# Whole tiles for the 16 left-over keys, and two heads side by side in the weighted sums of a stick-breaking attention

## The chip, the core and the metric

The kernel runs on one core of a Trainium2 chip. The metric is the device time of one execution in microseconds (us); lower is better. Engines are named as in the profile: PE is TensorE's matrix products, PEld its weight loads, DVE is VectorE, ACT is ScalarE, POOL is GpSimd and SP is SyncE.

## What is computed

The whole program is a small two-layer trunk: 16 learned meta tokens are put before 1024 positions, a gated delta-rule layer and a SwiGLU layer follow, then one shared key/value projection, a layer of stick-breaking attention with 16 heads of 64, another SwiGLU layer and a last norm. The change touches the attention alone:

```python
z = jnp.einsum('bhqd,bhkd->bhqk', q_blk, k) * scale          # 16 heads, L = 1040 keys
log_beta = jax.nn.log_sigmoid(z)
log_keep = jnp.where(visible, log_beta - z, 0.0)             # visible: key before query
log_w = log_beta + lax.cumsum(log_keep, axis=3, reverse=True) - log_keep
w = jnp.where(visible, jnp.exp(log_w), 0.0)
return jnp.einsum('bhqk,bhkd->bhqd', w, v)
```

The kernel uses that the weight of a key is a difference of two neighbouring products of "keep" factors. So it forms the running product P of sigmoid(-z) from the last key backwards, and sums P against differences of neighbouring values plus a bias, which gives the same output.

## The kernel before

**Units.** A pair is two heads (128 rows of channels). There are 8 pairs (`PAIRS`). Each pair has 16 units (`NU`): two heads h and 8 query blocks i of 128, in the order `UNITS`: for big in 7, 6, 5, 4, for each head, block big and then block 7 - big. So units with an even number are big and those with an odd number small. A unit has 16 + 128 (i + 1) keys: i + 1 whole blocks of 128 and 16 keys left over.

**What a unit goes through.** PE forms the scores of the unit (`scores`, three units ahead; lines L2025 and L2026 for the low and high parts of the keys, L2028 for the mask). ACT takes the sigmoid of them from PSUM (`kept`, L1112, into the tile kp). DVE scans kp into Pr (`scan`, L1589, a running product). PE turns Pr over, in blocks of 128 (`turn`, L2059 for whole blocks, L2061 for the 16 keys left over: an ordinary product with 16 columns of weights that moves the last 32 columns of the identity). ACT copies the turned blocks from PSUM banks 4 and 5 into PT (`take_turned`, L1122). PE sums them against the differences of the values in dV (`weigh`, L2078 for whole blocks, L2076 and L2081 for the 16 keys, with 16 rows), into bank 6 or 7. dV holds for each block 256 columns: head 0's 64, 128 zeros, head 1's 64. Each head multiplies with 128 columns of it, of which 64 are zeros, so both heads add into the same 128 partitions of the bank. When a half of the pair's 1024 queries is done, DVE adds the bias and takes it out (`outputs`, L1630).

**fp32 products.** Each fp32 product (L2059 excepted, which is a transposition) appears in the trace as two load and two product instructions.

**Order on PE.** `slot(U)` writes it out: turn the first group of unit U, scores of U + 3, turn the second group, weigh unit U - 1, turn the third group, and in three slots of each pair turn the next pair's values (L2044). Before slot 0 come the scores of units 0 to 2 and the last job of the query projection. ACT, DVE and POOL each have their own queue in order; semaphores tie them together (`t_z` scores, `t_kp` sigmoid, `t_p` scan, `t_tr` turned group, `t_ca` group copied, `t_pv` unit weighed, `t_ot` output taken, `t_zero` zeroing done).

**POOL.** Once a pair it splits the last result into a high part (L802) and a low part (L804), forms the differences of the next values (`value_steps`, L778 to L781), and makes the low parts of the next keys and queries for each head (`split_keys`, L765 and L767), which wait for ACT's high parts (L1094, L1095). ACT makes those after units 3 and 7. Before the first unit POOL stores the last query projection (L785), waits for all stores and zeroes the middle of dV (L797).

Of the kernel before, what the change touches and what calls it, by code (L numbers as in the profile page):

```python
# [20 lines left out]
META = 16  # L21
# [104 lines left out]
def trunk(nc, x, meta_tokens, gdn_norm_g, gdn_w_in, gdn_conv_w, gdn_a_log, gdn_dt_bias, gdn_onorm_g,  # L126
# [17 lines left out]
    with ctx:  # L144
# [49 lines left out]
        with ExitStack() as a:  # L194
            def att_x(name, shape, dt=F32):
                return a.enter_context(nc.sbuf_tensor(name, shape, dt))
            dvT0 = att_x("dvT0", [128, L])
            with ExitStack() as b:
                kraw0 = [b.enter_context(nc.sbuf_tensor(f"krawp{i}", [128, L], F32)) for i in range(2)]
            KL0 = [att_x(f"KLp{i}", [128, L], F32R) for i in range(2)]  # L200
            KH0 = [att_x(f"KHp{i}", [128, L], F32R) for i in range(2)]
            PrX0 = att_x("PrX0", [128, L])
# [7 lines left out]
            PrX1 = att_x("PrX1", [128, 528])  # L210
            att_x("bpad", [128, 288])
# [31 lines left out]
        with ExitStack() as a:  # L243
            def att(name, shape, dt=F32):
                return a.enter_context(nc.sbuf_tensor(name, shape, dt))

            def key_query(tag):

                with ExitStack() as b:
                    kr = [b.enter_context(nc.sbuf_tensor(f"kraw{tag}{i}", [128, L], F32)) for i in range(2)]  # L250
                return (kr, [att(f"KL{tag}{i}", [128, L], F32R) for i in range(2)],
                        [att(f"KH{tag}{i}", [128, L], F32R) for i in range(2)],
                        [att(f"QS{tag}{i}", [128, SEQ], F32R) for i in range(2)])
            oT = att("oT", [128, SEQ])
            kpS1 = att("kpS1", [128, 528])
            kpB0 = att("kpB0", [128, L])
            set_e = key_query("e")
            kpS0 = att("kpS0", [128, 528])
            PTb = att("PTb", [128, 1056])
            att("tpad", [128, 400])  # L260
# [3 lines left out]
            PrB = [att(f"PrB{i}", [128, L]) for i in range(2)]  # L264
            PrS = [att(f"PrS{i}", [128, 528]) for i in range(2)]
            kpB1 = att("kpB1", [128, L])
            PTs = att("PTs", [128, 544])
        gpad = keep("gpad", [128, 2 * L + 512])

        with ExitStack() as a:  # L270
# [93 lines left out]

            return dV12[j % 2] if j else dV0

        def kp_of(U):

            return ((kpB0, kpB1), (kpS0, kpS1))[U % 2][U // 2 % 2]

        def Pr_of(U):

            return (PrX0, PrX1)[U] if U < 2 else (PrB, PrS)[U % 2][U // 2 % 2]

        def PT_of(U):

            return (PTb, PTs)[U % 2]

        def q_bank(m, ch):

# [204 lines left out]
        def _(pool):  # L585
# [197 lines left out]
            for m in range(P_Q.jobs):  # L783
                pool.wait_ge(taken, TAKEN0[P_Q] + 2 * (m + 1))
                pool.dma_start(s_q[m], obuf[:, m % 2, 0:SEQ]).then_inc(stored[m % 2], 16)  # L785
                if m == 3:
                    pool.memset(dV0[:, :, 64:192], 0.0).then_inc(t_zero, 1)
                    value_steps(0)
                if m == 4:
                    split_keys(0, 0)  # L790
                if m == 5:
                    split_keys(0, 1)
            for b in range(2):
                pool.wait_ge(stored[b], 16 * 28)
            pool.wait_ge(mm_chunk, P_O.mm0)
            for d in dV12:
                pool.memset(d[:, :, 64:192], 0.0).then_inc(t_zero, 1)  # L797

            def result(j):

# [16 lines left out]
        def _(act):  # L817
# [286 lines left out]
            def kept(U):  # L1104

                z0, n = z_place(U)
                act.wait_ge(t_z, U + 1)
                if U == 3:
                    act.wait_ge(taken, TAKEN0[P_O])
                if U > 3:  # L1110
                    act.wait_ge(t_p, U - 3)
                act.activation(kp_of(U)[:, 0:n], PSf[:, z0:z0 + n], ACT.Sigmoid, scale=-0.125).then_inc(t_kp, 1)  # L1112

            def take_turned(U, g):

                k0, nb = TURNS[UNITS[U % NU][1]][g]
                n = TURN_NO["P", U, g]
                w = 128 * nb + (32 if n == last_turn(U) else 0)
                act.wait_ge(t_tr, n + 1)
                if U > 1:  # L1120
                    act.wait_ge(t_pv, U - 1)
                act.activation(PT_of(U)[:, 128 * k0:128 * k0 + w], PS[:, 4 + n % 2, 0:w], ACT.Copy).then_inc(t_ca, 1)  # L1122

            def take_values(j, g):

                k0, nb = V_PARTS[g]
                n = TURN_NO["V", j, g]
                rows = META if g == 2 else 128
                act.wait_ge(t_tr, n + 1)
                act.wait_ge(t_zero, 1 if j == 0 else 3)  # L1130
                if j > 2:
                    act.wait_ge(t_pv, NU * (j - 1))
# [52 lines left out]
        def _(dve):  # L1185
# [434 lines left out]

            def outputs(j, ch):

                dve.wait_ge(t_pv, NU * j + 16 - ch)
# [27 lines left out]
        def _(pe):  # L1651
# [396 lines left out]
            def turn(U, g):  # L2048

                i = UNITS[U % NU][1]  # L2050
                k0, nb = TURNS[i][g]
                n = TURN_NO["P", U, g]
                if n < 5:
                    pe.wait_ge(taken, TAKEN0[P_Q] + 2 * P_Q.jobs - 4 + n)
                pe.wait_ge(t_ca, n - 1)
                pe.wait_ge(t_p, U + 1)
                P = Pr_of(U)
                for k in range(nb):
                    m = pe.transpose(PS[:, 4 + n % 2, 128 * k:128 * k + 128], P[:, 128 * (k0 + k):128 * (k0 + k) + 128], ident[:, :])  # L2059
                if n == last_turn(U):  # L2060
                    m = pe.matmul(PS[0:META, 4 + n % 2, 128 * nb:128 * nb + 32], P[:, 128 * (i + 1):128 * (i + 1) + META],  # L2061
                                  ident[:, 96:128], start=True, stop=True)
                m.then_inc(t_tr, 1)

            def weigh(U):

                j, u = divmod(U, NU)
                h, i = UNITS[u]
                V, P = dV_of(j), PT_of(U)
# [13 lines left out]
                m.then_inc(t_pv, 1)  # L2083

            def slot(U):
# [102 lines left out]
```

## Time and profile before

| what | value |
|---|---|
| median of 3 runs | 3294.31 us (3293.29 to 3294.46) |
| the profiled execution | 3292.72 us |
| its span, first to last instruction | 3291.1 us |
| PE busy | 3196.3 us, 97% |
| DVE, ACT, POOL busy | 1601.5, 887.3, 657.0 us |
| mean granted TensorE clock | 0.993 |
| attention stage | 2035.8 to 2432.9 us |

The profile is that of one execution. Its matrix products are pipelined, and the ends of their records are modelled: a product of 128 columns has a record of some 0.27 us, though the next can start 0.11 us after it. What tells the pace is the distance from start to start.

### The profile page before, as it was taken

The numbers are of one execution on the slowest core, as the hardware profiler recorded it, in microseconds if no ns is written. First come the engines' busy times: TensorE is split into PE (matmuls) and PEld (weight loads), VectorE is DVE, ScalarE is ACT, GpSimd is POOL, SyncE is SP. The second block draws the span as 40 slices with busy tenths as digits, with TensorE's granted clock in tenths as the row PEclk, the third lists the DMA queues.
The fourth block names the chain that finished last, engine by engine and source line by source line (L and its number), as shares of the span: only waits on it lengthen the run. The fifth ranks groups of instructions, "written<-read, shape, count | busy, mean of one in ns | idle before, by whom it ended". The sixth has DMA issues, their size and how long they took to land.

```text
span 3291.1 us, 47938 instructions
## 1 busy us (share of the span) xinstructions
PE 3196.3 (97%) x19632; PEld 2904.9 (88%) x19632; DVE 1601.5 (49%) x2016; ACT 887.3 (27%) x1418; POOL 657.0 (20%) x558
## 2 busy tenths in 40 slices
PE   7999989999999999999998999999999999999998
PEld 6999978888899999999998997888888777777776
DVE  5777456666543334433345333676644334333343
ACT  3211245555421111111112002555532111111112
POOL 3000145555220100000002003344302000000000
PEclk9999999999999999999999999999999999999999
DMA  3333311111111111111111233212201111111111
GB/s 93 91 93 95 105 61 48 53 53 32 49 58 45 45 45 45 38 51 45 45 45 52 91 109 104 59 40 66 52 16 62 45 45 45 51 45 45 51 38 64
DMA packets 196954, 190.38 MB, mean 58 GB/s; under 512 B 7595, under 2 KB 171580, under 8 KB 196812
## 3 DMA queue, kind: packets, MB, share of 16 engines
q1 hardware_dynamic: 188748, 158.60, 16.4%
q0 software_dynamic: 8064, 29.76, 2.7%
q8 instruction: 105, 1.72, 0.2%
q14 instruction: 37, 0.30, 0.0%
HBM read 154.35 MB, written 33.98 MB: 57 GB/s over the span
## 4 chain that ended last, share of the span: by engine, by line
PE 95%; DVE 2%; ACT 2%; issue 1%; POOL 0%; DMA 0%; SPq 0%; ACTq 0%; DVEq 0%; POOLq 0%
PE PS L1659 18%; PE PS L1661 18%; PE PS L1660 18%; PE PS L1977 5%; PE PS L1975 5%; PE PS L1976 5%; PE PS L2078 5%; PE PS L1796 3%; PE PS L2059 2%; PE PS L1805 2%; PE PS L2025 1%; PE PS L2026 1%; PE PS L1812 1%; PE PS L1765 1%; PE PS L2076 1%
## 5 line engine op out<-in xcount | busy, mean ns | idle before, releaser
L1659 PE MATMUL PS<-YH,WL 128*128 128x348 f32 (+1 forms) x3040 | 1040.9, 342 | 14.8 <-DVE hT L1522 14.1
L1660 PE MATMUL PS<-YL,WH 128*128 128x348 f32 (+1 forms) x3040 | 1038.3, 342 | 0.0
L1661 PE MATMUL PS<-YH,WH 128*128 128x348 f32 (+1 forms) x3040 | 1037.4, 341 | 0.0
L1659 PEld LDWEIGHTS PS<-YH,WL 128*128 128x128 f32 x3040 | 571.5, 188 | 61.1 <-DVE hT L1522 19.0
L1660 PEld LDWEIGHTS PS<-YL,WH 128*128 128x128 f32 x3040 | 571.2, 188 | 37.4 <-issue 1.0
L1661 PEld LDWEIGHTS PS<-YH,WH 128*128 128x128 f32 x3040 | 572.4, 188 | 35.6
L749 POOL TENSOR_TENSOR gact<-gact,rs 128x346 f32<-128x346 f32 (+2 forms) x110 | 118.9, 1081 | 1326.3 <-ACT gact L1041 1326.3
L1522 DVE TENSOR_TENSOR hT<-PS,hT 128x346 f32<-128x346 f32 (+2 forms) x440 | 251.9, 586 | 189.2 <-PE PS L1977 189.2
L1975 PE MATMUL PS<-AH,WL 128*128 128x346 f32 (+2 forms) x880 | 310.4, 353 | 12.8 <-DVE AL L1512 6.4
L1976 PE MATMUL PS<-AL,WH 128*128 128x346 f32 (+2 forms) x880 | 310.3, 353 | 0.0
L1977 PE MATMUL PS<-AH,WH 128*128 128x346 f32 (+2 forms) x880 | 310.3, 353 | 0.0
L1047 ACT ACTIVATE AH<-aact 128x1040 fp32r<-128x1040 f32 (+1 forms) x44 | 47.0, 1067 | 866.2 <-DVE aact L1509 866.2
L1189 DVE TENSOR_TENSOR WL<-raw,WH 128x1024 fp32r<-128x1024 f32 x204 | 250.2, 1244 | 46.4 <-ACT WH L821 44.9
L1509 DVE TENSOR_TENSOR aact<-PS,gact 128x346 f32<-128x346 f32 (+2 forms) x110 | 64.7, 588 | 419.4 <-PE PS L1661 419.4
L1975 PEld LDWEIGHTS PS<-AH,WL 128*128 128x128 f32 x880 | 166.6, 189 | 29.2 <-issue 7.1
L1589 DVE TENSOR_TENSOR_SCAN PrB<-kpB 128x912 f32<-128x912 f32 (+3 forms) x63 | 156.4, 2482 | 73.1 <-ACT kpB L1112 73.1
L1977 PEld LDWEIGHTS PS<-AH,WH 128*128 128x128 f32 x880 | 166.8, 190 | 15.7
L1976 PEld LDWEIGHTS PS<-AL,WH 128*128 128x128 f32 x880 | 166.8, 189 | 15.7
L1499 DVE TENSOR_TENSOR gact<-PS,rs 128x346 f32<-128x346 f32 (+2 forms) x110 | 64.5, 586 | 223.8 <-PE PS L1661 223.7
L821 ACT ACTIVATE WH<-raw 128x1024 fp32r<-128x1024 f32 x148 | 150.8, 1047 | 33.1 <-DMA raw<-in_ffn_w_gate_up 30.4
L1041 ACT ACTIVATE gact<-gact 128x346 f32<-128x346 f32 (+2 forms) x110 | 60.4, 549 | 321.8 <-DVE gact L1499 321.6
L666 POOL TENSOR_TENSOR LT<-NT,lvl 104x416 f32<-104x416 f32 x120 | 132.0, 1125 | 0.0
(273 smaller groups left out, 4406.2 us busy)
## 6 DMA issues: line engine op xcount, KB each, us to landing
raw<-in_ffn_w_gate_up SPq DMA_DIRECT2D x88, 512.0 KB, 3.7
raw<-in_ffn_w_down SPq DMA_DIRECT2D x44, 512.0 KB, 3.6
s_in<-obuf POOLq DMA_DIRECT2D x32, 520.0 KB, 4.4
raw<-in_gdn_w_in SPq DMA_DIRECT2D x32, 512.0 KB, 4.0
Xqk<-s_in SPq DMA_DIRECT2D x10, 832.0 KB, 4.3
s_kv<-obuf POOLq DMA_DIRECT2D x16, 520.0 KB, 4.1
raw<-in_w_kv SPq DMA_DIRECT2D x16, 512.0 KB, 4.0
qraw<-s_q SPq DMA_DIRECT2D x32, 256.0 KB, 6.7
```

The costliest lines, as they stand in the source:

```text
L666: pool.tensor_tensor(by_head(LT[g][:, (k - 1) % LTB, :]), by_head(NT[c % 2][g][:, :]), lvl[:, k, :].unsqueeze(1).broadcast_to([C, HG, C]), ...
L821: act.activation(WH[s][:, :], raw[s][:, :], ACT.Copy).then_inc(w_hi, 1)
L1189: dve.tensor_tensor(WL[s][:, :], raw[s][:, :], WH[s][:, :].bitcast(F32), ALU.subtract).then_inc(w_lo, 1)
L1522: dve.tensor_tensor(dst, PS[:, banks[u % len(banks)], 0:n], dst, ALU.add).then_inc(d_add, 1)
L1589: dve.tensor_tensor_scan(Pr_of(U)[:, 0:n][:, ::-1], kp, kp, 1.0, ALU.mult, ALU.bypass).then_inc(t_p, 1)
L1659: pe.matmul(PS[:, bank, 0:n], wl, xh, start=(k == 0), stop=False)
L1660: pe.matmul(PS[:, bank, 0:n], wh, xl, start=False, stop=False)
L1661: m = pe.matmul(PS[:, bank, 0:n], wh, xh, start=False, stop=(k == KT - 1))
L1975: pe.matmul(bank, wl, ah, start=(t == 0), stop=False)
L1976: pe.matmul(bank, wh, al, start=False, stop=False)
L1977: y = pe.matmul(bank, wh, ah, start=False, stop=(t == 1))
L2078: m = pe.matmul(PS[:, bank, c0:c0 + 128], V[:, k, 128 * h:128 * h + 128], P[:, 128 * k:128 * k + 128], start=(h == 0 and k == 0), stop=(h ...
```

## The change

It has four parts. In `turn` the 16 keys left over are transposed as a whole block of 128 (the tiles P are now 640 and 1152 columns wide, so that it exists; only 16 rows and 32 columns of the result are used, which `take_turned` copies by an instruction of its own). In `weigh` the two heads of a query block are taken together, once the second head's unit is there: 64 calls instead of 128. Head h is a column tile of 64 at `tile_position` (0, 64 h), with 64 columns of weights, and writes 64 partitions; the heads alternate for each key block. The left-over keys are summed there with all 128 rows of dV and PT, whose rows beyond 16 POOL has zeroed. `slot` calls `weigh` only for U - 1 of 2 and 3 modulo 4. kp and Pr become one tile, scanned in place, and PT gets a buffer for each head.

```diff
         def take_turned(U, g):
-                w = 128 * nb + (32 if n == last_turn(U) else 0)
                 act.wait_ge(t_tr, n + 1)
-                if U > 1:
-                    act.wait_ge(t_pv, U - 1)
-                act.activation(PT_of(U)[:, 128 * k0:128 * k0 + w], PS[:, 4 + n % 2, 0:w], ACT.Copy).then_inc(t_ca, 1)
+                if U > 3:
+                    act.wait_ge(t_pv, U // 4 * 2 - 1 + U % 2)
+                if n == last_turn(U):
+                    act.wait_ge(t_zero, 6)
+                    act.activation(PT_of(U)[0:META, tail_of(U):tail_of(U) + 32], PS[0:META, 4 + n % 2, 128 * nb + 96:128 * nb + 128], ACT.Copy)
+                act.activation(PT_of(U)[:, 128 * k0:128 * (k0 + nb)], PS[:, 4 + n % 2, 0:128 * nb], ACT.Copy).then_inc(t_ca, 1)
...
         def kept(U):
-                if U == 3:
-                    act.wait_ge(taken, TAKEN0[P_O])
                 if U > 3:
-                    act.wait_ge(t_p, U - 3)
-                act.activation(kp_of(U)[:, 0:n], PSf[:, z0:z0 + n], ACT.Sigmoid, scale=-0.125).then_inc(t_kp, 1)
+                    act.wait_ge(t_tr, last_turn(U - 4) + 1)
+                act.activation(P_of(U)[:, 0:n], PSf[:, z0:z0 + n], ACT.Sigmoid, scale=-0.125).then_inc(t_kp, 1)
...
         def scan(U):
                 dve.wait_ge(t_kp, U + 1)
-                if U > 3:
-                    dve.wait_ge(t_tr, last_turn(U - 4) + 1)
-                kp = kp_of(U)[:, 0:n][:, ::-1]
-                dve.tensor_tensor_scan(Pr_of(U)[:, 0:n][:, ::-1], kp, kp, 1.0, ALU.mult, ALU.bypass).then_inc(t_p, 1)
+                P = P_of(U)[:, 0:n][:, ::-1]
+                dve.tensor_tensor_scan(P, P, P, 1.0, ALU.mult, ALU.bypass).then_inc(t_p, 1)
...
         def turn(U, g):
                 if n == last_turn(U):
-                    m = pe.matmul(PS[0:META, 4 + n % 2, 128 * nb:128 * nb + 32], P[:, 128 * (i + 1):128 * (i + 1) + META],
-                                  ident[:, 96:128], start=True, stop=True)
+                    m = pe.transpose(PS[:, 4 + n % 2, 128 * nb:128 * nb + 128], P[:, 128 * (i + 1):128 * (i + 2)], ident[:, :])
...
         def weigh(U):
                 pe.wait_ge(t_ca, last_turn(U) + 1)
-                if u < 2 and j:
-                    pe.wait_ge(t_ot, 4 * j - 2 + 2 * u)
+                if u < 4 and j:
+                    pe.wait_ge(t_ot, 4 * j - 2 + 2 * (u % 2))
                 for k in range(i + 1):
-                    if h and k == i:
-                        pe.matmul(PS[:, bank, c0 + 96:c0 + 128], V[0:META, i + 1, 128:256], P[0:META, 128 * i + 128:128 * i + 160],
-                                  start=False, stop=False)
-                    m = pe.matmul(PS[:, bank, c0:c0 + 128], V[:, k, 128 * h:128 * h + 128], P[:, 128 * k:128 * k + 128],
-                                  start=(h == 0 and k == 0), stop=(h == 1 and k == i))
-                if not h:
-                    m = pe.matmul(PS[:, bank, c0 + 96:c0 + 128], V[0:META, i + 1, 0:128], P[0:META, 128 * i + 128:128 * i + 160],
-                                  start=False, stop=False)
+                    for h in range(2):
+                        pe.matmul(PS[64 * h:64 * h + 64, bank, c0:c0 + 128], V[:, k, 192 * h:192 * h + 64],
+                                  P[h][:, 128 * k:128 * k + 128], start=(k == 0), stop=False, tile_position=(0, 64 * h))
+                for h in range(2):
+                    m = pe.matmul(PS[64 * h:64 * h + 64, bank, c0 + 96:c0 + 128], V[:, i + 1, 192 * h:192 * h + 64],
+                                  P[h][:, r0:r0 + 32], start=False, stop=True, tile_position=(0, 64 * h))
                 m.then_inc(t_pv, 1)
...
         def slot(U):
-                if U:
+                if U and (U - 1) % 4 > 1:
                     weigh(U - 1)
```

On POOL, the zeroing before the attention now also covers the last 32 columns of the four PT tiles and the whole last block of each dV, and it comes before the wait for the stores. The waits for `t_pv` in `take_values` and `outputs` count 8 weighings a pair instead of 16.

## Rows read from the trace of the kernel before

**Rows 1.** The page: the span, and the chain that ended last.

```profile
span 3291.1 us, 47938 instructions
...
PE 95%; DVE 2%; ACT 2%; issue 1%; POOL 0%; DMA 0%; SPq 0%; ACTq 0%; DVEq 0%; POOLq 0%
```

**Rows 2.** Stretches: us; busy PE, PEld, DVE, ACT, POOL (instructions); clock, DMA share, GB/s.

```profile
2278.80:2328.50 49.70, 49.70 (x365) 41.29 (x364) 33.20 (x21) 26.79 (x52) 20.03 (x10) 1.00 0.23 52
...
2378.20:2432.90 54.70, 54.70 (x399) 45.49 (x399) 28.09 (x24) 26.32 (x52) 3.44 (x2) 1.00 0.09 23
```

**Rows 3.** Waits, 2079.8 to 2378.2 us: us in total, times, longest.

```profile
DVE oT L1630 <- PE PS L2078: 27.3, 6, 4.6
```

**Rows 4.** PE in order of time: start, us, line, operation, tiles, shape, count.

```profile
2294.06 0.44 PE L2059 MATMUL PS<-ident,PrB 128*128 128x128 f32 x2
...
2294.59 0.33 PE L2059 MATMUL PS<-ident,PrS 128*128 128x128 f32 x1
2294.85 0.23 PE L2061 MATMUL PS<-ident,PrS 128*16 128x32 f32 x2
2295.01 0.50 PE L2025 MATMUL PS<-KLo,QSo 128*128 128x512 f32 x1
2295.35 0.39 PE L2026 MATMUL PS<-KHo,QSo 128*128 128x512 f32 x1
2295.58 0.34 PE L2025 MATMUL PS<-KLo,QSo 128*128 128x400 f32 x1
...
2296.01 1.78 PE L2078 MATMUL PS<-PTb,dV 128*128 128x128 f32 x14
2297.72 0.40 PE L2076 MATMUL PS<-PTb,dV 16*128 16x32 f32 x2
2298.05 0.49 PE L2078 MATMUL PS<-PTb,dV 128*128 128x128 f32 x2
```

**Rows 5.** The weight loads of the same stretch.

```profile
2294.85 0.11 PEld L2061 LDWEIGHTS PS<-ident,PrS 128*16 128x16 f32 x2
...
2295.94 1.65 PEld L2078 LDWEIGHTS PS<-PTb,dV 128*128 128x128 f32 x14
```

**Rows 6.** Order of time on PE at the value block of 16.

```profile
2322.69 0.27 PE L2044 MATMUL PS<-ident,dvT 128*16 128x128 f32 x1
2322.80 0.60 PE L2059 MATMUL PS<-ident,PrB 128*128 128x128 f32 x4
```

**Rows 7.** Order of time on PE in the first layer.

```profile
641.58 1.63 PE L1863 MATMUL PS<-osq,ones 128*128 128x416 f32 x4
643.05 0.88 PE L1812 MATMUL PS<-ident,U 104*104 104x104 f32 x8
```

**Rows 8.** Order of time on DVE and POOL, undisturbed first, then together.

```profile
2037.11 2.33 DVE L1589 TENSOR_TENSOR_SCAN PrB<-kpB 128x1040 f32<-128x1040 f32 x1 [1.60 <-ACT kpB L1112]
2039.35 0.43 DVE L1589 TENSOR_TENSOR_SCAN PrS<-kpS 128x144 f32<-128x144 f32 x1
...
2044.42 1.92 POOL L778 TENSOR_TENSOR dvT<-vT 128x1039 f32<-128x1039 f32 x1 [2.72 <-DMA vT<-s_kv]
...
2289.83 1.06 POOL L802 CAST XH<-oT 128x1024 fp32r<-128x1024 f32 x1 [23.40 <-DVE oT L1630]
2290.97 2.35 POOL L804 TENSOR_TENSOR XL<-oT,XH 128x1024 fp32r<-128x1024 f32 x1
2291.26 3.98 DVE L1589 TENSOR_TENSOR_SCAN PrB<-kpB 128x912 f32<-128x912 f32 x1 [1.20 <-ACT kpB L1112]
2293.29 3.67 POOL L778 TENSOR_TENSOR dvT<-vT 128x1039 f32<-128x1039 f32 x1
...
2299.57 2.40 POOL L765 TENSOR_TENSOR KLe<-krawe,KHe 128x1040 fp32r<-128x1040 f32 x1
2302.05 2.66 POOL L767 TENSOR_TENSOR QSe<-qraw,QSe 64x1024 fp32r<-64x1024 f32 x1
```

**Rows 9.** Instruction groups by shape from 2278.8 to 2328.5 us.

```profile
L1122 ACT ACTIVATE PTs<-PS 128x160 f32<-128x160 f32 x5 | 1.5, 301 | 0.0
```

More of the change, by code:

```diff
@@ L201, in trunk @@
             KH0 = [att_x(f"KHp{i}", [128, L], F32R) for i in range(2)]
-            PrX0 = att_x("PrX0", [128, L])
+            att_x("ppad", [128, L])
             vT = att_x("vT", [128, L])
@@ L254, in trunk @@
             oT = att("oT", [128, SEQ])
-            kpS1 = att("kpS1", [128, 528])
-            kpB0 = att("kpB0", [128, L])
+            att("rpad", [128, 16])
+            PB = [att("PB0", [128, 1152]), None]
+            att("epad", [128, 400])
             set_e = key_query("e")
-            kpS0 = att("kpS0", [128, 528])
-            PTb = att("PTb", [128, 1056])
-            att("tpad", [128, 400])
+            Psm = [att("PS0", [128, 640]), None]
+            PTb = [att("PTb0", [128, 1056]), None]
+            att("tpad", [128, 288])
             set_o = key_query("o")
@@ L263, in trunk @@
             dV12 = [att(f"dV{i}", [128, 9, 256]) for i in range(2)]
[L264 to L267, printed above, removed]
+            PB[1] = att("PB1", [128, 1152])
+            Psm[1] = att("PS1", [128, 640])
+            PTb[1] = att("PTb1", [128, 1056])
+            PTs = [att(f"PTs{i}", [128, 544]) for i in range(2)]
         gpad = keep("gpad", [128, 2 * L + 512])
@@ L365, in dV_of, with P_of, tail_of @@
             return dV12[j % 2] if j else dV0
[L367 to L373, printed above, removed]
+        def P_of(U):
+            return (PB, Psm)[U % 2][U // 2 % 2]
         def PT_of(U):
-            return (PTb, PTs)[U % 2]
+            return (PTb, PTs)[U % 2][U // 2 % 2]
+        def tail_of(U):
+            return 512 if U % 2 else 1024
         def q_bank(m, ch):
@@ L786, in _ @@
                 if m == 3:
-                    pool.memset(dV0[:, :, 64:192], 0.0).then_inc(t_zero, 1)
+                    pool.memset(dV0[:, 0:8, 64:192], 0.0).then_inc(t_zero, 1)
+                    pool.memset(dV0[:, 8, :], 0.0).then_inc(t_zero, 1)
                     value_steps(0)
@@ L792, in _ @@
                     split_keys(0, 1)
+            pool.wait_ge(mm_chunk, P_O.mm0)
+            for h in range(2):
+                pool.memset(PTb[h][:, 1024:1056], 0.0).then_inc(t_zero, 1)
+                pool.memset(PTs[h][:, 512:544], 0.0).then_inc(t_zero, 1)
+            for d in dV12:
+                pool.memset(d[:, 0:8, 64:192], 0.0).then_inc(t_zero, 1)
+                pool.memset(d[:, 8, :], 0.0).then_inc(t_zero, 1)
             for b in range(2):
                 pool.wait_ge(stored[b], 16 * 28)
-            pool.wait_ge(mm_chunk, P_O.mm0)
-            for d in dV12:
-                pool.memset(d[:, :, 64:192], 0.0).then_inc(t_zero, 1)
             def result(j):
@@ L1129, in take_values @@
                 act.wait_ge(t_tr, n + 1)
-                act.wait_ge(t_zero, 1 if j == 0 else 3)
+                act.wait_ge(t_zero, 2 if j == 0 else 10)
                 if j > 2:
-                    act.wait_ge(t_pv, NU * (j - 1))
+                    act.wait_ge(t_pv, NU // 2 * (j - 1))
                 act.activation(dV_of(j)[0:rows, k0:k0 + nb, :].rearrange("p k (q c) -> p k q c", c=64)[:, :, 0:4:3, :],
@@ L1621, in outputs @@
             def outputs(j, ch):
-                dve.wait_ge(t_pv, NU * j + 16 - ch)
+                dve.wait_ge(t_pv, NU // 2 * j + 8 - ch)
                 if j:
@@ L2056, in turn @@
                 pe.wait_ge(t_p, U + 1)
-                P = Pr_of(U)
+                P = P_of(U)
                 for k in range(nb):
@@ L2067, in weigh @@
                 j, u = divmod(U, NU)
-                h, i = UNITS[u]
-                V, P = dV_of(j), PT_of(U)
+                i = UNITS[u][1]
+                V, P, r0 = dV_of(j), (PT_of(U - 2), PT_of(U)), tail_of(U)
                 bank, c0 = 6 + i // 4, 128 * (i % 4)
                 pe.wait_ge(t_ca, last_turn(U) + 1)
-                if u < 2 and j:
-                    pe.wait_ge(t_ot, 4 * j - 2 + 2 * u)
+                if u < 4 and j:
+                    pe.wait_ge(t_ot, 4 * j - 2 + 2 * (u % 2))
                 for k in range(i + 1):
-                    if h and k == i:
-                        pe.matmul(PS[:, bank, c0 + 96:c0 + 128], V[0:META, i + 1, 128:256], P[0:META, 128 * i + 128:128 * i + 160],
-                                  start=False, stop=False)
-                    m = pe.matmul(PS[:, bank, c0:c0 + 128], V[:, k, 128 * h:128 * h + 128], P[:, 128 * k:128 * k + 128],
-                                  start=(h == 0 and k == 0), stop=(h == 1 and k == i))
-                if not h:
-                    m = pe.matmul(PS[:, bank, c0 + 96:c0 + 128], V[0:META, i + 1, 0:128], P[0:META, 128 * i + 128:128 * i + 160],
-                                  start=False, stop=False)
+                    for h in range(2):
+                        pe.matmul(PS[64 * h:64 * h + 64, bank, c0:c0 + 128], V[:, k, 192 * h:192 * h + 64],
+                                  P[h][:, 128 * k:128 * k + 128], start=(k == 0), stop=False, tile_position=(0, 64 * h))
+                for h in range(2):
+                    m = pe.matmul(PS[64 * h:64 * h + 64, bank, c0 + 96:c0 + 128], V[:, i + 1, 192 * h:192 * h + 64],
+                                  P[h][:, r0:r0 + 32], start=False, stop=True, tile_position=(0, 64 * h))
                 m.then_inc(t_pv, 1)
```

3 lines of the change are left out of this document (1 added, 2 removed).

## The prediction

> **What bounds the kernel now.** I read the page first: the chain that ended last is 95% TensorE (PE) over a span of 3291.1 us, so no other engine sets the end [rows 1]. The profiled execution took 3292.7 us, 1.6 less than the median of 3294.3 us, and the sum below is made against the former. Then I cut out the attention stage, which is all that the diff touches. One pair of heads lasts 49.7 us; PE is busy for all 49.7 of it, VectorE (DVE) for 33.2, ScalarE (ACT) for 26.8, GpSimd (POOL) for 20.0, and the granted clock is 1.00, the upper level of 2.4 GHz [rows 2]. Eight such pairs fill the time from 2035.8 to 2432.9 us. In the list of waits PE waits for nobody there; DVE waits for PE, about 4.6 us once a pair, before it takes the sums out [rows 3]. So a nanosecond less on PE is a nanosecond less of time, until the next engine is in the way. The second row there is the last pair, in which POOL prepares nothing for a next one.
>
> A busy PE need not be PE at its peak, so I went on to single starts on PE. A plain value product of 128 columns of weights goes every 0.112 us: 14 loads in 1.65 us, the last 0.19 long [rows 4, 5]. The short products for the 16 left-over keys are the surprise. On the value side, from 2296.01 to 2298.05 there are 14 plain products and one tail of two 32-column instructions: 2.04 us, where 14 x 0.112 is 1.57. The next two products take 0.49 us to the end of the last, whose record is 0.27 long, so the step between them is 0.22 instead of 0.11. Of these 0.58 us some 0.05 belongs to the mask product ahead; 0.53 is the tail's. Where transpositions follow, the exit is 0.05 cheaper (two in 0.44, less the last one's 0.27, is 0.17 instead of 0.11), so the mean is 0.5 us [rows 4]. On the transposition side one transposition with its 128*16 tail takes 0.42 us instead of 0.11, of which some 0.05 comes from the tail before; the 512-column product behind it takes 0.34 instead of 0.23. That is about 0.36 us a tail [rows 4]. Two instructions of 16 weight columns are only 0.04 us of work, so each of the two changes of shape costs about 0.16 us. A transposition with 16 columns of weights pays nothing: the next starts 0.11 us later [rows 6]. It is the change of array shape by an ordinary product that costs, not the small operand.
>
> **The change, part by part.** There are 128 units (8 pairs x 2 heads x 8 query blocks).
>
> Turned tails: 128 x 0.36 = 46 us go, 128 whole transpositions at 0.11 = 14 us come. Gain 32 us.
>
> Value tails: 128 x 0.5 = 64 us go. In their place stand 64 weighings, each entering and leaving the two-tile shape: 2 x 0.16 = 0.32 us. Each also holds four short tail instructions (two heads, two passes of the fp32 product). Loads of 16 columns stand 0.015 us apart (two in 0.11, one 0.09) and those of 128 stand 0.112 [rows 5], so I take 0.056 for 64 columns, 0.22 us for the four. 64 x 0.54 = 35 us. Gain 29 us.
>
> Value products: 8 x 72 x 2 = 1152 instructions before and after, 129 us at 0.112. No row shows two column tiles at once. The upper bound is that they run one after another. Streaming 128 fp32 columns costs about 0.11 us whatever is loaded: 416 fp32 columns take 1.47/4 = 0.37 us, while 512 columns of the rounded type take 0.23 [rows 4, 7]. Then nothing is gained. The lower bound is that two stream together and the loads set the pace, 0.056 us each by the estimate above, so 64.5 us go. I take the lower one: outputs and weight columns of the two heads are disjoint, the loads balance it exactly, and the end hardly depends on it, as the next part shows.
>
> TensorEngine Tiling (Array Packing) of the Trainium skill, section Key Properties, says that changing the tiling mode drains the array, while different tiles run in parallel. Its first half agrees with the 0.16 us above; the second no run here shows. By it the products are worth the 64.5 us, by the serial row 0; and a change of tile inside a weighing costs nothing.
>
> On PE that is 32 + 29 + 64.5 = 126 us, 15.7 a pair: 49.7 becomes 34.0. Without overlap it is 61 us, 7.6 a pair: 42.1.
>
> **What is late next.** A scan of 1040 columns takes 2.33 us and one of 144 takes 0.43, so 2.12 ns a column plus 0.12. The 2 x 8 scans of a pair (9472 columns) need 22.1 us. Scans and POOL's operations exclude each other. The scan of 912 columns needs 2.05 us by that rate; it is issued at 2291.26, lasts 3.98, and ends 2.0 us after POOL's subtraction ends at 2293.32. POOL's next one needs 1.92 us alone, but lasts 3.67 when queued behind that scan [rows 8]. POOL's own work a pair is 2.35 + 1.9 + 2 x 2.4 + 2 x 2.66 + 1.06 + about 0.6 = 16 us [rows 8] (1.06 is the conversion, 0.6 my estimate of its three small operations; what is left of the 20.0 busy in [rows 2] are waits for scans). Together 38.1 us, and 39.6 with the 1.5 us in which DVE takes sums out. That is the floor once PE needs only 34.0. Scores run only three units before their transpositions, so idle time of one side is not all made up later. I take 40.0 us for each of the six middle pairs, a gain of 9.7, together 58 us. The first has neither the 3.4 us of result conversion nor its first two scans: gain 11 (34.0 plus some 4 of waits). The last has POOL nearly empty: gain 13 (34.0 plus 2 to 3 of waits). 82 us in all.
>
> SBUF — State Buffer of the Trainium skill, section SBUF: two separate sides, says that GpSimd and a VectorE operation with two SBUF inputs hold a shared port exclusively, for a whole instruction. The trace agrees: a scan of 2.05 us lasts 3.98. It speaks against the change: by it about 44 of the 126 us that PE saves come to nothing.
>
> Costs that I set at nothing. ACT gets one more copy of 32 columns for each unit. A copy of 160 columns takes 0.30 us [rows 9]; 0.2 by the least, so net 2.7 us a pair, 29.5 of 40: hidden beside PE and DVE. Queued behind it are the main copy, and PE's transposition two banks on. In the slots that no longer hold a weighing (two of four) PE has only scores to cover the copy; I count up to 0.4 us there, in the 40.0 and the first and last pair's waits. Ridding the kernel of separate scan outputs moves a wait: the sigmoid now waits for the transpositions of four units earlier, which PE has done a slot before. The new zeroing of the tails comes ahead of the zeroing of dV on POOL and is small; ACT's first tail copy needs it at about 2038.5 us. If it is late, that costs some 1 us once. The longer weighings delay DVE's taking out of sums by less than the 4.6 us that it now waits.
>
> **The rivals.**
> A (my forecast): PE at 34, DVE and POOL bound the middle pairs. 3292.7 - 82 + 1.6 = 3212 us. For it: full use of PE, the port rows. By the bounds of the middle pairs, 38.5 to 43 us, it is 3203 to 3230. Chance 0.58.
> B: the two tiles don't overlap. PE at 42.1 is above the floor; 42.5 with small waits, 7.2 x 8 = 58 us: 3236 us, 3229 to 3245. For it: no row shows overlap, and fp32 products take two passes. Against it: nothing in the trace. 0.25.
> C: the port binds less, because POOL's operations fall where PE has DVE idle anyway, or its records overstate them. A pair takes 36 us, 13.7 x 8 = 110: 3184 us. Against it: 22.1 + 16 has to be placed in it. 0.08.
> D, the other side: each change of tile inside a weighing costs like a change of shape. A pair has 36 key blocks and 8 tails, each with a step to the other head and one back, so 88 changes; at 0.16 us they cost 14.1 us against 7.6 gained: a pair takes 56.2 us, and the time is 3294.3 + 8 x 6.5 = 3346 us. It decides from 7.6/88 = 0.086 us a change. For it: the rows price a change at twice that. Against it: the array keeps its shape between the two heads. 0.06.
> The remaining 0.03 is for a wait that I don't see that takes it all.
>
> **How the numbers follow.** The forecast is A's 3212 us. A and B together hold 0.83, so the range reaches from a little below A's lower bound to B's upper bound: 3195 to 3245 us. A measurement here tells no less than about 0.2% (6.6 us) from no change. Faster by more: A, B, C and a little more, 0.93; within: 0.01; slower: D, 0.06.
>
> **What would show it.** Transposition tails gone as a shape, one more transposition of 128 for each unit at 0.11 us. Value products: starts of both heads in pairs and 0.056 us apart in the mean (A), or 0.11 (B), or over 0.16 (D). One gap of some 0.1 us before and after each of 64 weighings. PE waits for scans, 5 us a pair in the middle pairs under A, next to none under B. DVE near or over 33 us busy in 40. The period of a middle pair is 40.0 (A), 42.5 (B), 36 (C). I am wrong if PE waits for ACT's copies in the slots without a weighing, far above 0.4 us each, or if the granted clock falls below 1.00 once PE has waits in it.

## The result, and the profile after

The changed kernel takes 3194.45 us (median of 4 runs, 3194.15 to 3194.66) against 3294.39 us of the kernel before on the same chip: 0.9697 of it, with a 95% interval of 0.968 to 0.9714. That is 99.9 us less. The forecast was 3212 us, in a range from 3195 to 3245: the direction held, and what came to bind the middle pairs was what I had foretold, though it cost less than I had put it at. The time lies 0.55 us below the range.

The page of the changed kernel, its span and its chain, to be laid beside [rows 1]:

```profile
span 3192.5 us, 47692 instructions
...
PE 89%; DVE 6%; ACT 2%; issue 1%; DMA 1%; POOL 0%; SPq 0%; ACTq 0%; DVEq 0%; POOLq 0%
```

DVE now has 6% of the chain, where it had 2%. Two stretches of the changed kernel, a middle pair and the last, with the columns of [rows 2]:

```profile
2186.20:2223.40 37.20, 34.09 (x347) 28.48 (x347) 34.09 (x20) 26.51 (x69) 24.90 (x10) 1.00 0.31 74
...
2297.90:2333.00 35.10, 32.48 (x338) 27.21 (x340) 27.00 (x22) 23.65 (x66) 5.14 (x2) 1.00 0.14 33
```

A middle pair takes 37.2 us instead of 49.7. PE and DVE are both busy for 34.1 of them (for DVE that includes its waits for POOL), so neither works without a gap: they hand the wait to and fro. Cut at the first transposition of a pair, the stage compares as follows (starts from the order of time on PE; the last pair ends with the last sums taken out):

| stretch | before | after | gain | forecast gain |
|---|---|---|---|---|
| first pair | 51.1 | 42.3 | 8.8 | 11 |
| six middle pairs | 6 x 49.7 | 6 x 37.2 | 75 | 58 |
| last pair | 48.9 | 35.1 | 13.8 | 13 |

The products of the value sums on PE in order of time, which answer to [rows 4]:

```profile
2197.05 0.34 PE L2029 MATMUL PS<-KHe,QSe 128*128 128x400 f32 x1
2197.23 0.23 PE L2031 MATMUL PS<-maskb,identb 128*128 128x128 bf16 x1
2197.39 1.97 PE L2078 MATMUL PS<-PTb,dV 128*64 128x128 f32 x32
2199.18 0.26 PE L2081 MATMUL PS<-PTb,dV 128*64 128x32 f32 x4
2199.37 0.33 PE L2062 MATMUL PS<-ident,PB 128*128 128x128 f32 x1
```

There are 32 products in 1.97 us, the last record 0.28 long: 0.055 us a product, half of the 0.112 of [rows 4, 5]. The first comes 0.16 us after the mask product, where it came 0.07 after it in [rows 4] with no change of shape (the row of 2296.01 and the load of 2295.94): 0.09 for going into column tiles. The four tail instructions and the way out take 0.19 us together.

DVE and POOL of the changed kernel in order of time, which answer to [rows 8]:

```profile
2195.06 2.06 DVE L1592 TENSOR_TENSOR_SCAN PB<-PB 128x912 f32<-128x912 f32 x1 [0.73 <-ACT PB L1115]
2197.03 2.83 DVE L1592 TENSOR_TENSOR_SCAN PS<-PS 128x272 f32<-128x272 f32 x1
2199.79 3.70 DVE L1592 TENSOR_TENSOR_SCAN PB<-PB 128x912 f32<-128x912 f32 x1
2203.41 0.69 DVE L1592 TENSOR_TENSOR_SCAN PS<-PS 128x272 f32<-128x272 f32 x1
2204.03 1.76 DVE L1592 TENSOR_TENSOR_SCAN PB<-PB 128x784 f32<-128x784 f32 x1
```

```profile
2194.10 1.06 POOL L807 CAST XH<-oT 128x1024 fp32r<-128x1024 f32 x1 [12.00 <-DVE oT L1633]
2195.24 4.04 POOL L809 TENSOR_TENSOR XL<-oT,XH 128x1024 fp32r<-128x1024 f32 x1
2199.24 2.34 POOL L778 TENSOR_TENSOR dvT<-vT 128x1039 f32<-128x1039 f32 x1
2201.55 1.96 POOL L779 TENSOR_SCALAR dvT<-vT 128x1 f32<-128x1 f32 x1
2203.46 0.64 POOL L780 COPY bias<-vT 128x8 f32<-128x8 f32 x1
2204.04 1.73 POOL L781 COPY bias<-vT 128x8 f32<-128x8 f32 x1
```

They take turns, as foretold: the subtraction of 2195.24 doesn't get on before the scan ends at 2197.12, the next scan waits for it until 2199.28, and so on. And PE waits for it:

```profile
2202.28 0.23 PE L2031 MATMUL PS<-maskb,identb 128*128 128x128 bf16 x1
2203.64 0.41 PE L2062 MATMUL PS<-ident,PB 128*128 128x128 f32 x2 [1.12 <-DVE PB L1592]
```

The transposition needs the scan that ends at 2203.49, 3.70 us after its issue. But two things in the rows of DVE and POOL were not in my sum. An operation that had to wait takes 0.12 to 0.2 us less once it may run than it takes alone: the subtraction ends 2.16 us after the scan (alone 2.35), the next ends 1.7 us after its scan (alone 1.92), the scan of 2199.79 ends 1.91 us after the subtraction (alone 2.05). I read it as its start overlapping the other's end. And the three small operations hold nobody up: they wait for scans themselves (those of 2201.55, 2203.46 and 2204.04 each end within 0.02 us of a scan), but the scans of 2203.41 and 2204.03 run at their own pace with a POOL operation in flight.

The conversion does take turns. It starts at 2194.10, in the middle of a scan that lasts from 2193.88 to 2194.33, and ends 0.83 us after that scan; in a kernel of the experiments below (two of POOL's operations twice) one starts with no scan in flight and takes 1.04 us, and the scan that is issued in the middle of it ends 1.91 us after it:

```profile
2205.30 1.04 POOL L811 CAST XH<-oT 128x1024 fp32r<-128x1024 f32 x1 [10.34 <-DVE oT L1640]
2205.94 2.31 DVE L1599 TENSOR_TENSOR_SCAN PB<-PB 128x912 f32<-128x912 f32 x1 [0.73 <-ACT PB L1122]
```

In the changed kernel it costs next to nothing all the same, as DVE waits 0.73 us for ACT's sigmoid just then, from 2194.33 to 2195.06.

### The profile page after: what moved, and what is told of

Same layout as the page of the kernel before. It is cut to its first block, busy times and chain, and to the rows that moved or that the text cites. A ratio compares the mean times of both kernels' runs of the same rounds, so it can differ in the third digit from the quotient of the medians.

```text
span 3192.5 us, 47692 instructions
## 1 busy us (share of the span) xinstructions
PE 3072.3 (96%) x19504; PEld 2804.0 (88%) x19504; DVE 1606.5 (50%) x2016; ACT 885.2 (28%) x1546; POOL 687.9 (22%) x565
## 4 chain that ended last, share of the span: by engine, by line
PE 89%; DVE 6%; ACT 2%; issue 1%; DMA 1%; POOL 0%; SPq 0%; ACTq 0%; DVEq 0%; POOLq 0%
PE PS L1662 19%; PE PS L1664 19%; PE PS L1663 19%; PE PS L1980 5%; PE PS L1978 5%; PE PS L1979 5%; PE PS L1799 3%; DVE PB L1592 2%; PE PS L1808 2%; DVE PS L1592 2%; PE PS L2062 1%; PE PS L1815 1%; PE PS L2078 1%; PE PS L1768 1%; PE PS L2029 1%
## 5 line engine op out<-in xcount | busy, mean ns | idle before, releaser
L1592 DVE TENSOR_TENSOR_SCAN PB<-PB 128x1040 f32<-128x1040 f32 (+3 forms) x64 | 158.1, 2470 | 20.4 <-ACT PB L1115 20.4
L826 ACT ACTIVATE WH<-raw 128x1024 fp32r<-128x1024 f32 x148 | 150.8, 1047 | 35.1 <-DMA raw<-in_ffn_w_gate_up 32.4
```

Of the source, the lines that this page charges most:

```text
L826: act.activation(WH[s][:, :], raw[s][:, :], ACT.Copy).then_inc(w_hi, 1)
L1592: dve.tensor_tensor_scan(P, P, P, 1.0, ALU.mult, ALU.bypass).then_inc(t_p, 1)
```

## The experiments

Each pair below is a middle pair. The same pieces of the program ahead of the attention ended up to 4 us apart from kernel to kernel, so a few us between kernels are not to be believed without the lengths of the pairs. Every experiment was timed beside the kernel before on its own chip (medians of 3292.9 to 3295.1 us), and the changed kernel again only beside the last group; the first four and the doubled operations have two executions each.

**One head after the other.** The same instructions in another order:

```diff
-                for k in range(i + 1):
-                    for h in range(2):
+                for h in range(2):
+                    for k in range(i + 1):
```

> The changed kernel, but in each weighing all blocks of head 0 come first and then all of head 1; the same instructions, tiles and sums. Theory 1 (the gain of the value products is that two neighbouring instructions for different column tiles stream together): starts 0.11 us apart instead of 0.055 in the mean, 144 x 0.055 = 7.9 us more on PE a pair, PE from 33 to 41, above what else binds; a middle pair goes from 37.2 to about 41.2 us and the time from 3194 to about 3227 us. Rival 1 (64 columns of weights make an instruction cheap by themselves, or PE fetches the other tile's instructions from far ahead): no change, 3194 us.

Measured: 3236.5 us, 0.9827 of before (0.9799 to 0.9856), a middle pair 42.3 us. That is 9 us above the expectation of 3227: PE is busy for 38.8 us of the pair, less than the 41 expected, but 3.5 us of waits stand beside them. The order of time on PE in this kernel:

```profile
2176.89 3.00 PE L2078 MATMUL PS<-PTb,dV 128*64 128x128 f32 x29
2179.62 0.30 PE L2081 MATMUL PS<-PTb,dV 128*64 128x32 f32 x2
2179.72 0.49 PE L2078 MATMUL PS<-PTb,dV 128*64 128x128 f32 x3
2180.05 0.25 PE L2081 MATMUL PS<-PTb,dV 128*64 128x32 f32 x2
```

32 products take 3.16 us, 0.10 each. So the gain of the column tiles is that neighbours in the queue for different tiles stream together; a tile of 64 columns alone is worth next to nothing: away from the seam its starts are 0.109 us apart. The step is a little under 0.11, because around the seam between the heads some still overlap: the tail of head 0, which stands behind all of head 1's blocks in the program, starts before head 1's last three records.

**Without column tiles.** Whole tiles stay for the left-over keys, and so does the new order of the weighings; each head multiplies with 128 columns of weights again:

```diff
-                        pe.matmul(PS[64 * h:64 * h + 64, bank, c0:c0 + 128], V[:, k, 192 * h:192 * h + 64],
-                                  P[h][:, 128 * k:128 * k + 128], start=(k == 0), stop=False, tile_position=(0, 64 * h))
+                        pe.matmul(PS[:, bank, c0:c0 + 128], V[:, k, 128 * h:128 * h + 128],
+                                  P[h][:, 128 * k:128 * k + 128], start=(h == 0 and k == 0), stop=False)
...
-                    m = pe.matmul(PS[64 * h:64 * h + 64, bank, c0 + 96:c0 + 128], V[:, i + 1, 192 * h:192 * h + 64],
-                                  P[h][:, r0:r0 + 32], start=False, stop=True, tile_position=(0, 64 * h))
+                    m = pe.matmul(PS[:, bank, c0 + 96:c0 + 128], V[:, i + 1, 128 * h:128 * h + 128],
+                                  P[h][:, r0:r0 + 32], start=False, stop=(h == 1))
```

> The changed kernel without column tiles: both heads multiply with 128 columns of weights, 64 of them zeros, as before the change; the whole tiles for the left-over keys and the order of the weighings stay. It isolates the first half of the change. By the steps in the traces 144 x 0.112 + 32 x 0.11 = 19.6 us of weighing a pair instead of 11.2, PE 33 + 8.4 = 41.4, a middle pair about 41.6 us, the time about 3230 us. So some 64 of the 100 us would come from the whole tiles alone, and 36 from the column tiles. Rival: the shape changes of the old tails were hidden somewhere and the tails are worth little; then this is near 3270 us.

Measured: 3250.9 us, 0.9871 of before (0.9842 to 0.9899). Its middle pair:

```profile
2169.40:2213.50 44.10, 42.32 (x347) 38.23 (x347) 32.89 (x20) 26.68 (x69) 22.78 (x10) 1.00 0.26 61
```

The whole tiles, with the new order of the weighings, are worth 42 us, and the column tiles 56 more; the expectation had 64 and 36, and 3230 us. PE's own work came out 0.9 us a pair above it, and 1.8 us of waits come on top, most of them of transpositions for ACT's copies. I put them down to the slots that have lost their weighing; that was not tested by itself.

**POOL's subtractions taken away.** For each of the four:

```diff
-                pool.tensor_tensor(KL[b][:, :], kr[b][:, :], KH[b][:, :].bitcast(F32), ALU.subtract).then_inc(t_lo, 1)
+                pool.memset(KL[b][:, :].bitcast(F32), 0.0).then_inc(t_lo, 1)
```

> The changed kernel with POOL's four kinds of subtraction in the attention (low parts of keys, queries and results, differences of values) replaced by zeroing of the same tiles, which reads nothing; that part of the computation is left out. Theory 2 (scans and POOL's operations exclude each other, and this is what middle pairs wait for now): scans have no long records any more, PE waits little, a middle pair about 34 us, 3194 - 6 x 3.2 = 3175 us. Rival 2 (the waits of PE come from ACT's copies and the order of slots): a middle pair stays at 37 us, 3194 us.

Measured: 3181.2 us, 0.9659 of before (0.9631 to 0.9687), 13 us below the changed kernel. Its middle pair:

```profile
2180.00:2215.00 35.00, 33.83 (x347) 28.37 (x347) 23.15 (x20) 26.37 (x69) 7.69 (x10) 1.00 0.32 78
```

DVE falls from 34.1 to 23.2 us busy, without one scan less: 10.9 us of its records were waits for POOL. PE has 33.8 us of work, as forecast (34.0), and 1.2 us idle. So in the changed kernel taking turns costs 2.2 us a middle pair, where the forecast had PE wait for scans for 5.

**Value products taken away.** Only the first key block of each sum is multiplied.

```diff
-                for k in range(i + 1):
+                for k in range(1):
```

> The changed kernel with only the first block of each sum multiplied; the other blocks' value products are left out. PE has 112 x 0.055 = 6.2 us less a pair, 27 instead of 33. Theory 2: the middle pairs are at the port's floor and hardly move: 35 to 37 us, 3180 to 3194 us; what they come to is the floor that I put at 38.1. Rival (PE sets the pace of most of the pair): 31 us a pair, 3145 us.

Measured: 3189.4 us, 0.9684 of before (0.9656 to 0.9712). The middle pairs take 36.3 to 38.8 us, 37.5 in the mean, against 37.2 in the changed kernel. Two of its rows:

```profile
2110.10:2147.40 37.30, 30.96 (x235) 24.85 (x235) 34.60 (x20) 26.76 (x69) 23.47 (x10) 0.91 0.31 72
...
2297.80:2331.70 33.90, 30.50 (x250) 24.25 (x251) 29.33 (x27) 25.95 (x71) 5.08 (x2) 1.00 0.14 34
```

A middle pair doesn't get shorter with less work on PE. It is a weaker proof than it looks: the granted clock of this stretch is 0.91, so PE spent part of it at the lower level of 1.2 GHz, after it had waited. What it shows, as the changed kernel does, is that a pair of 37.3 us is possible with POOL's work in it, so the floor of 38.1 us was no floor. It also shows the conversion taking turns, in every pair:

```profile
2117.15 1.06 POOL L807 CAST XH<-oT 128x1024 fp32r<-128x1024 f32 x1 [13.43 <-DVE oT L1633]
2117.55 2.57 DVE L1592 TENSOR_TENSOR_SCAN PB<-PB 128x912 f32<-128x912 f32 x1 [0.17 <-ACT PB L1115]
```

The scan is issued in the middle of the conversion and ends 1.91 us after it, the same as behind a subtraction.

**Two of POOL's operations twice.**

```diff
+                pool.tensor_tensor(XL[:, j, META:L], oT[:, :], XH[:, j, META:L].bitcast(F32), ALU.subtract).then_inc(t_x, 1)
+                tx[0] += 1
+                pool.wait_ge(t_x, tx[0])
                 pool.tensor_tensor(XL[:, j, META:L], oT[:, :], XH[:, j, META:L].bitcast(F32), ALU.subtract).then_inc(t_ol, 1)
```

(and likewise for the differences of the values)

> The changed kernel with two of POOL's operations done twice in each pair, with the same result: the low part of the result (2.35 us) and the differences of the values (1.9 us). Theory 2 (middle pairs are bound by scans and POOL's operations taking turns): nearly all of the 4.0 us that this adds to their sum shows, a middle pair 41 us, 3194 + 6 x 3.9 = 3218 us. Rival (PE's 33.8 us and the waits for ACT bind, POOL's work is mostly beside it): under 1.5 us a pair, at most 3203 us.

Measured: 3220.6 us (3217.6 and 3223.6), 0.9778 of before (0.9758 to 0.9798). The six middle pairs take 40.3 to 41.5 us, 41.0 in the mean: 3.8 us more for 4.3 us of added work (2.35 and 1.92 alone; 2.16 and 1.7 behind a scan). At the margin, POOL's work in a middle pair is paid nearly in full.

**The second pair's high parts later.** In the changed kernel's first pair ACT stands still ahead of the first conversion of the second pair's keys, and all its later work waits behind it:

```profile
2049.35 1.07 ACT L1099 ACTIVATE KHo<-krawo 128x1040 fp32r<-128x1040 f32 x1 [5.13 <-DMA qraw<-s_q]
```

Three stretches of the changed kernel there show what follows:

```profile
2046.00:2050.00 4.00, 1.05 (x14) 0.77 (x13) 0.31 (x1) 0.65 (x1) 2.49 (x4) 1.00 1.03 220
2050.00:2054.00 4.00, 2.09 (x8) 1.79 (x9) 1.83 (x1) 3.02 (x8) 2.47 (x2) 0.64 1.04 206
2054.00:2058.00 4.00, 4.00 (x18) 3.52 (x18) 3.29 (x2) 2.93 (x7) 2.59 (x1) 0.50 0.18 67
```

PE has next to nothing to do, and then the granted clock falls to the lower level, 0.50 (1.2 GHz), and stays there for 4 us in which PE is busy throughout.

```diff
-                    if u in (3, 7):
-                        split_keys(j + 1, u // 4)
+                    if u in ((3, 7) if j else (7, 10)):
+                        split_keys(j + 1, int(u > (3 if j else 7)))
```

> The changed kernel, in which ACT makes the high parts of the second pair's keys and queries after units 7 and 10 of the first pair instead of 3 and 7. In the first pair of the changed kernel DVE waits 5.9 us for a sigmoid behind ACT's wait for the loads of these keys. Theory 3 (this wait, and the lower clock after it, ate some 5 us of the first pair's gain): the gap goes and the first pair takes 5 to 8 us less, 3187 to 3190 us. Rival (the loads are late whatever waits for them, and the next pair takes up the delay): within 2 us of 3194 us.

Measured: 3190.5 us (3187.6 to 3192.0), 0.9683 of before (0.9667 to 0.97). The first pair goes from 42.3 to 35.9 us, with the clock at 1.00. Of these 6.4 us the time shows 4.0, and this kernel's profile 2.2: its first transposition came 4.2 us later. That lateness is not the edit's work. It is there in the kernel with one head after the other too, which lacks the edit (first transposition at 2040.72 us, against 2036.28 in the changed kernel), and most of it arises long before the attention: from 1720 to 1730 us PE is busy throughout in all three kernels, at a granted clock of 1.00 in the changed kernel and of 0.76 and 0.77 in these two. Why the clock differs there is open.

**Both weighings in one slot.**

```diff
-                if U and (U - 1) % 4 > 1:
-                    weigh(U - 1)
+                if U % 4 == 3:
+                    weigh(U - 1)
+                    weigh(U)
```

> The changed kernel, in which both weighings of four units stand next to each other in the slot of the fourth unit, so that PE changes into column tiles and back once instead of twice: 32 entries and exits of 0.25 to 0.3 us less, 1.1 us a pair. If the middle pairs are bound by scans and POOL (theory 2), nearly nothing shows: 3190 to 3195 us. If PE's own work sets the pace, 3185 us.

Measured: 3202.1 us, 0.9722 of before (0.9706 to 0.9738), 7.7 us more than the changed kernel. Both expectations missed. The change of shape in between does go (the second weighing starts 0.09 us after the first's tails), but a middle pair takes 38.4 us. I put it down to three slots of four that have no weighing under which ACT's copies and DVE's scans can catch up. Two of its waits:

```profile
PEld PS L2062 <- ACT PTb L1127: 15.7, 36, 0.8
...
PEld PS L2062 <- ACT dV L1138: 12.2, 10, 1.4
```

In the changed kernel the first is 10.1 us over six pairs, and the second is not in the list. But a turn is lost as well:

```profile
2198.43 2.36 POOL L809 TENSOR_TENSOR XL<-oT,XH 128x1024 fp32r<-128x1024 f32 x1
2198.44 4.26 DVE L1592 TENSOR_TENSOR_SCAN PB<-PB 128x912 f32<-128x912 f32 x1 [0.93 <-ACT PB L1115]
```

Here the subtraction starts 0.01 us before the scan and goes first, and the scan lasts 4.26 us; in the changed kernel the scan comes first and lasts 2.06. Which of the two makes the 1.2 us was not separated.

**Low parts on DVE.**

```diff
+                if j < PAIRS - 1 and u in (7, 11):
+                    low(j + 1, u // 8)
```

Here `low` holds the two subtractions of `split_keys`, on DVE, and POOL's calls for the later pairs are gone.

> The changed kernel with the low parts of keys and queries of the later pairs made by DVE (after the scans of units 7 and 11) instead of POOL. A subtraction of 1024 columns takes DVE 1.24 us and POOL 2.4 to 2.7 us, so the sum of what excludes each other falls by 10.1 - 5.0 = 5 us a pair, from 33.4 to about 28.5, below PE's 33.8. Theory 2: a middle pair comes near PE's own pace as with the zeroings in place of the subtractions, 35 us, 3194 - 6 x 2.2 = 3181 us. Rival (what counts is DVE's own work, not the exclusion): DVE gets 5 us more to do, a middle pair stays at 37 us or grows, 3194 us or more.

Measured: 3190.1 us, 0.9685 of before (0.9668 to 0.9701), a middle pair 36.5 us: a third of what I expected. The order of time points to a reason. The subtractions that stay on POOL are those that come when PE is closest behind DVE, and the two scans behind them are as long as in the changed kernel:

```profile
2195.12 2.83 DVE L1590 TENSOR_TENSOR_SCAN PS<-PS 128x272 f32<-128x272 f32 x1
2197.88 3.70 DVE L1590 TENSOR_TENSOR_SCAN PB<-PB 128x912 f32<-128x912 f32 x1
```

If so, it is not the sum of the turns that binds the pair, but the two scans behind the result's low part and the value differences. The next version tests it.

**Everything on DVE.** All four subtractions of the later pairs are on DVE: the result's after the scan of unit 5, the value differences after unit 6, the low parts of keys and queries after units 7 and 11 (10 and 13 in the first pair), together with the later high parts. Beside it, the previous kernel with the later high parts alone, and the changed kernel again.

> The changed kernel with all four kinds of subtraction of the later pairs on DVE, which needs 1.2 us for each where POOL needs 1.9 to 2.7, and with the second pair's high parts made later as in e5_late_split. POOL keeps the conversion and three small operations. Theory 2: nothing but scans and DVE's own work is left on the port, so a middle pair comes to the 35.0 us of e3_memsets, and with the first pair's 3 to 5 us the time is 3176 to 3181 us, below the changed kernel and below the kernel before. Rival (a scan that stands behind a subtraction on DVE is as late as one that waits for POOL): 36.5 us as in e9_dve_low, 3187 us.

> e9_dve_low with the second pair's high parts made later as in e5_late_split. If the two gains add (3.9 and 4.3 us), 3186 us; if the 4 us of e5_late_split were scatter from kernel to kernel, 3190 us.

> The changed kernel itself, on the same chip as the two above: 3194 us within 2. The stage ahead of the attention ends between 2022 and 2027 us in the traces so far, for kernels that are the same there; this shows how much of a few us between kernels is worth believing.

Measured, five rounds on one chip:

| kernel | median us | ratio to before | first, middle, last pair |
|---|---|---|---|
| changed kernel again | 3194.43 | 0.9699 (0.9686 to 0.9712) | 40.9, 37.2, 35.1 |
| low parts of keys and queries on DVE, later high parts | 3184.27 | 0.9667 (0.9654 to 0.9681) | 34.8, 36.5, 35.1 |
| all four on DVE, later high parts | 3175.92 | 0.9640 (0.9626 to 0.9653) | 34.8, 35.0, 35.1 |

A middle pair of the last:

```profile
2185.00:2220.00 35.00, 33.83 (x347) 28.36 (x347) 29.45 (x26) 26.33 (x68) 4.82 (x5) 1.00 0.33 77
```

The pair is as short as with the subtractions left out, though they are all done. This version beats both kernels, by 119 and 18.5 us. It does what the expectation said of theory 2, and the rival there (a subtraction on DVE delays a scan as much) is out: it delays it for 1.2 us only. The version changes two things at once, though, the engine of the two remaining subtractions and their place in the order; whether later turns on POOL would have done as well was not tested.

## Why the prediction was right in kind and outside its range

**What bounds the kernel before**: right. PE's own work set the pace of the attention, and each shape change in it was paid.

**PE's work after**: right in sum, 33.8 us a pair in the two kernels without subtractions on POOL against 34.0 forecast, and nearly so in its halves: the left-over keys gave 7.4 us a pair (49.7 to 42.3) where I had 7.6, the value products 8.5 (42.3 to 33.8) where I had 8.1. The four short tail instructions cost less than the 0.22 us that I gave them: with the way out of column tiles they take 0.19.

**Overlap of two column tiles**: right. The lower bound, 0.056 us, was taken and 0.055 measured; the experiment with one head after the other shows that it is the order of the queue that makes it. Rival B is out: it would have needed 42.1 us of PE work a pair. Rival D is out too: no product waits for a change of tile.

TensorEngine Tiling (Array Packing) of the Trainium skill, section Key Properties, says that a change of mode drains the array and that different tiles run in parallel. Both halves are in line with the runs: 0.09 us more on entry, and 0.055 us a product.

**What is late next**: right in kind, and wrong in size. This is the step that failed. I wrote "Together 38.1 us, and 39.6 with the 1.5 us in which DVE takes sums out. That is the floor", and took 40.0 for a middle pair, with 38.5 as the lower bound. It was 37.2. The sum added times that operations take alone, or with a wait in them, and the rows show less. Take for each operation of DVE and POOL in the pair from 2186.20 us only what it adds: from its start, or from the end of the one before it where that is later, to its own end. Then the scans take 20.4 us where I had 22.1, the six subtractions 12.7 where I had 14.4, the conversion 0.8 of 1.06, the small operations nothing where I had 0.6, the taking out of the sums 1.4 of 1.5. That is 35.3 us against the 39.6, and 1.9 us in which neither engine is at work make the 37.2. Whoever stands behind another, of either engine, is 0.1 to 0.2 us quicker: that is most of the scans' and the subtractions' part.

Some of it could be read in [rows 8] before the run. The scan of 2291.26 ends 1.92 us after the subtraction, at 2295.24 against 2293.32; I wrote 2.0, and missed that this is less than the 2.05 it takes alone. The differences behind it end 1.72 us after it, and not 1.92. And the 2.66 us that I took twice as the queries' subtraction have a wait in them: behind a scan in the changed kernel it takes 2.16 to 2.18.

Six pairs at 2.8 us less than forecast are 17 us of the 18 that were missed, and the last pair 0.8; the first pair took back 2.2, and the other 2 lie outside the three rows of the table. And the sum alone doesn't tell the length: counted in the same way it is 31.8 us with the low parts on DVE, but a pair took 36.5, and only the version that also moved the other two subtractions freed the rest. A sum of exclusive work bounds a pair from below; what it costs above PE's time depends on when each turn comes.

**The lower end of the range**: rival C, with the port binding less, was given 36 us a pair and 8%; the truth lies between A and C, nearer to C, and half of C's reason is what the rows bear out: the records overstate what POOL's operations hold. The range left C out and began at 3195 us. That the time came within 0.55 us of it is luck: without the 2.2 us that the first pair lost it would have been further off.

**The first pair**: forecast gain 11, measured 8.8. The wait of ACT for the loads of the second pair, 5.1 us, and the fall of the clock after it were not in the working, though in the kernel before, too, DVE starts no scan from 2046.6 to 2051.9 us. One of my signs of being wrong came true there, and not in the middle pairs: the granted clock fell below 1.00 (0.92 over the first pair) once PE had waits in it.

**The costs set at nothing**: the zeroing on POOL was done by 2037.96 us, in time. ACT's additional copies have records of 0.17 us and stayed beside PE; ACT is busy for 26.5 us of a middle pair, not for 29.5 as forecast. Of the slots without a weighing I wrote up to 0.4 us; with subtractions out of the way all waits of PE in a pair are 1.2 us. The merged weighings cost 1.2 us a pair more, though there a lost turn comes in beside the cover.

## What to carry to other kernels

Put instructions for different column tiles next to each other in the queue; behind one another they gain next to nothing. Keep small left-over products in the array shape of their neighbours, zero-padded, since on PE each change of shape costs more than the padding. When the engine that sets the pace is relieved, look for work of two engines that takes turns, add only what each operation takes behind the other, and look first at the operation that comes when the follower is closest, not at the longest one.

## What the runs showed of the hardware that was not expected

- PE lets a later instruction for an idle column tile start before earlier ones for the busy tile: head 0's tail ran before head 1's last three products, and 32 products in the serial order took 0.10 us each, not 0.11.
- A DVE or POOL operation that waited for the other needs 0.12 to 0.2 us less after it than alone (2.16 instead of 2.35, 1.91 instead of 2.05).
- POOL's conversion of 128x1024 takes turns with scans like its subtractions (a scan issued in it ends 1.91 us after it). Its zeroing doesn't: with it in the place of the subtractions DVE's busy time falls from 34.1 to 23.2 us. Copies of 8 columns wait for scans, up to 1.73 us, and hold none up.
- The same subtraction of some 1024 columns takes DVE 1.2 us and POOL 2.4 us, and a small POOL copy issued beside DVE's waits for its 1.2 us; moved to DVE it halves what it takes from the two together.
- After PE had been idle for most of 4 us in the first pair, the granted clock fell to 0.50 and stayed there over 4 us of unbroken work. In the kernel with fewer products PE is busy for 2.2 us from 2084 to 2088 us at 1.00, and over the next 4 us the granted clock is 0.53; in the middle pairs of the changed kernel it stayed at 1.00.
